# Rotary tables interleaved with two mixers, router logits moved into the layer norm, and smaller retention buffers

## The reference

```python
u = h @ ev_w_in[j]                       # layer 0: xa, ya | q, k, v, g
out_a = rg_lru_mixer(xa, ya, ...)        # conv, gates, scan over positions, gelu branch
out_b = retention_mixer(q, k, v, g, positions, gn_w)
...
def retention_mixer(q, k, v, g, positions, gn_w):
    q = rotary(q, positions); k = rotary(k, positions) * (RET_DIM ** -0.5)   # cos, sin of positions * inv_freq
    ...                                  # per head: chunk scores with decay, state recurrence over chunks
    o = head_group_norm(from_chunks(o_intra + o_inter), gn_w, RET_HEADS)
    return jax.nn.silu(g) * o
...
h = layer_norm(DEEPNORM_ALPHA * h + mix, ln_mix_g[i], ln_mix_b[i])
def hierarchical_moe(x, ...):
    group_logits = t @ w_group + b_group             # 4 columns
    expert_logits = einsum('td,gde->tge', t, w_router) + b_router    # 16 columns
    ...                                  # gate: one group, two of its four experts, softmax
```

## Time and profile before

| | us |
|---|---|
| median of six runs | 4342.27 (4284.7 to 4551.81) |
| the profiled execution | 4286.33 |
| its span on the slowest core (core 3) | 4284.8 |
| spans of the eight cores | 4266.7 to 4284.8 |
| load of x, layer 0 | 0 to 38 |
| rotary tables | 38 to 86 |
| loads, layer 0's mixers | 86 to 704 |
| reload of x, output projection and layer norm | 704 to 925 |
| router | 925 to 1024 |
| experts of layer 0 | 1024 to 1716 |
| router of layer 1 | 3228 to 3328 |

### The profile page before, as it was taken

How to read it: one execution, slowest core, us unless ns; L and a number is a source line. 1 busy time by engine, 2 the same in 40 slices (tenths; PEclk the granted TensorE clock), 3 DMA queues, 4 the chain that set the end, 5 groups by cost and what they waited for, 6 DMA issues and landing times.

```text
span 4284.8 us, 40588 instructions; the slowest of 8 cores (4266.7 to 4284.8 us)
## 1 busy us (share of the span) xinstructions
PE 2712.2 (63%) x12672; PEld 1312.2 (31%) x12672; DVE 1790.9 (42%) x2953; ACT 1173.3 (27%) x1880; POOL 1046.5 (24%) x857
## 2 busy tenths in 40 slices
PE   2544434619999999356534335555535999999646
PEld 1221222206444444122311112222215444444213
DVE  4233333322555555254432423333141455555344
ACT  1243332221111111342313125555230111111233
POOL 0323431131223232220123321111031223232130
PEclk6766766857999999678655556666765999999868
DMA  4010113020323231212000011001402122323201
GB/s 105 7 15 5 15 10 89 10 31 1 45 30 45 30 45 16 44 40 61 6 0 5 0 11 10 1 10 10 98 0 31 22 39 34 41 32 44 45 1 79
DMA packets 167293, 124.61 MB, mean 29 GB/s; under 512 B 62224, under 2 KB 143888, under 8 KB 166960
## 3 DMA queue, kind: packets, MB, share of 16 engines
q0 software_dynamic: 134352, 73.69, 13.6%
q1 hardware_dynamic: 32736, 48.33, 3.7%
HBM read 178.90 MB, written 16.78 MB: 46 GB/s over the span
## 4 chain that ended last, share of the span: by engine, by line
PE 54%; DVE 13%; DMA 9%; ACT 9%; POOL 8%; issue 7%; DVEq 0%; ACTq 0%; POOLq 0%; SPq 0%
PE psb L250 52%; POOL lnt L274 4%; DVE lnt L274 2%; ACT L270 2%; PE psb L254 2%; DMA ptok<-p 1%; DVE ssd_tmp L299 1%; DMA w_out<-od_w_out 1%; DMA xtok<-x 1%; POOL CdT L274 1%; DVE hg_kvall L299 1%; DMA wr_102<-moe_w_router 1%; DMA wr_255<-moe_w_router 1%; POOL MIX L274 1%; DMA wv<-ev_w_in 1%
## 5 line engine op out<-in xcount | busy, mean ns | idle before, releaser
L274 DVE TENSOR_TENSOR R<-R,psb 128x512 f32<-128x512 f32 x1088 | 664.5, 678 | 117.6 <-PE psb L250 117.6
L274 POOL TENSOR_TENSOR hm<-tm,gB 128x512 bf16<-128x512 f32 x256 | 325.5, 1271 | 1164.9 <-DVE tm L274 1164.9
L250 PE MATMUL psb<-HB,w1e 128*128 128x512 bf16 x2048 | 488.0, 381 | 0.0
L250 PE MATMUL psb<-HB,w3e 128*128 128x512 bf16 x2048 | 483.8, 379 | 0.0
L250 PE MATMUL psb<-hm,w2e 128*128 128x512 bf16 x2048 | 462.6, 379 | 0.0
L250 PEld LDWEIGHTS psb<-HB,w3e 128*128 128x128 bf16 x2048 | 200.4, 98 | 242.0 <-issue 0.7
L250 PEld LDWEIGHTS psb<-hm,w2e 128*128 128x128 bf16 x2048 | 200.4, 98 | 241.6
L250 PEld LDWEIGHTS psb<-HB,w1e 128*128 128x128 bf16 x2048 | 190.4, 98 | 242.9 <-issue 32.8
L274 POOL TENSOR_TENSOR lnt<-lnt,nmr 128x512 f32<-128x512 f32 x128 | 161.4, 1261 | 393.2 <-DVE lnt L274 393.2
L270 ACT ACTIVATE gB<-psb 128x512 f32<-128x512 f32 x128 | 76.4, 597 | 613.6 <-PE psb L250 613.6
L270 ACT ACT_TABLE_LOAD x136 | 174.5, 1283 | 179.5 <-PE psb L250 88.2
(11 more groups left out here) (381 smaller groups left out, 4172.7 us busy)
## 6 DMA issues: line engine op xcount, KB each, us to landing
xtok<-x SPq DMA_DIRECT2D x32, 512.0 KB, 5.5
w1e<-moe_w POOLq DMA_DIRECT2D x32, 512.0 KB, 6.1
w3e<-moe_w POOLq DMA_DIRECT2D x32, 512.0 KB, 8.8
w2e<-moe_w POOLq DMA_DIRECT2D x32, 512.0 KB, 11.2
r_spill<-R SPq DMA_DIRECT2D x4, 2048.0 KB, 7.3
R<-r_spill SPq DMA_DIRECT2D x4, 2048.0 KB, 34.8
out<-otok SPq DMA_DIRECT2D x16, 512.0 KB, 2.7
ptok<-p SPq DMA_DIRECT2D x32, 128.0 KB, 2.2
```

The costliest lines, as they stand in the source:

```text
L250: return self.op("pe", lambda e: e.matmul(out.ap, lhsT=lhsT.ap, rhs=rhs.ap, start=start, stop=stop), reads=[lhsT, rhs], writes=[out])
L274: return self.op(eng, lambda e: e.tensor_tensor(out=out.ap, in0=in0.ap, in1=in1.ap, op=op), reads=[in0, in1], writes=[out])
```

## The change

The rotary tables become a generator, `rotary_gen`, in four quarters of 512 tokens with 9 steps each, without a phase. `mixer_ret_gen` starts with it, so its 36 steps take turns with the first 36 steps of the LRU, and retention's own loads and heads come after them. To make room, `xb16`, `o_t` and `t3` become single tiles, and `sg` (2048 columns) goes: the g projection and its Silu move from the q and k loop into `_ret_gn`, one token tile at a time. The router's loads move ahead of `outproj_ln` (`router_setup`), and its matmuls into that pipeline, tile j-2 behind `ln_apply` of tile j-2 (`router_logits`); `moe_route` begins with the gate.

```diff
+def rotary_gen(self):
+    k = self.k
+    HS = SEQ // 4
+    self.cosT = k.sb([128, SEQ], F32, 4, "cosT")
+    self.sinT = k.sb([128, SEQ], F32, 4, "sinT")
...
+    for half in range(4):
+        hs = slice(half * HS, (half + 1) * HS)
+        k.dma("sp", posi.h[:], self.d["pos"][:, hs].partition_broadcast(128), writes=[posi.v()])
+        k.copy(ang.v(), posi.v())
+        k.ts(ang.v(), ang.v(), self.pcol("inv_freq"), ALU.mult)
+        yield
+        for shift, dst_t in ((math.pi / 2.0, self.cosT), (0.0, self.sinT)):
...
+            k.act(dst, dst, AF.Sin)
+            if dst_t is self.sinT:
+                k.ts(dst, dst, self.pcol("sin_sign"), ALU.mult)
+            yield
...
 def mixer_ret_gen(self):
...
+    yield from self.rotary_gen()
...
-    xb16 = [k.sb([128, 512], BF16, 1, "xb16") for _ in range(2)]
+    xb16 = [k.sb([128, 512], BF16, 1, "xb16")] * 2
...
-    sg = k.sb([128, SEQ], BF16, 4, "sg")
-    o_ts = [k.sb([128, 512], F32, 1, "o_t") for _ in range(2)]
+    sg = (k.sb([128, 512], BF16, 1, "sgj"), wg)
+    o_ts = [k.sb([128, 512], F32, 1, "o_t")] * 2
...
-            ps = self.proj(wg, 0, j)
-            k.act(sl(sg, j), ps.v(), AF.Silu)
...
     k.tt(c.v(), c.v(), b.v(), ALU.mult, eng="pool")
-    k.stt(self.MIXv(4 + hd, j), c.v(), self.pcol("ret_gnw", hd), sg.v(sg.h[:, j * 512:(j + 1) * 512], j), ALU.mult, ALU.mult)
+    sgj, wg = sg
+    ps = self.proj(wg, 0, j)
+    k.act(sgj.v(), ps.v(), AF.Silu)
+    k.stt(self.MIXv(4 + hd, j), c.v(), self.pcol("ret_gnw", hd), sgj.v(), ALU.mult, ALU.mult)
...
             self.ln_apply(j - 2, g, b, ga, ba, tmp)
+            self.router_logits(j - 2)
...
+def router_logits(self, j):
+    k = self.k
+    wr, bias, L = self.router_st
+    for tt in range(4 * j, 4 * j + 4):
         ps = k.ps()
         for kc in range(8):
             k.mm(ps.v(ps.h[:, 0:20]), self.R.v(self.R.h[:, kc, tt * 128:(tt + 1) * 128], self.rs(kc, tt // 4)),
                  wr.v(wr.h[:, kc, :]), start=(kc == 0), stop=(kc == 7))
-        k.stt(L.v(L.h[:, tt, :]), ps.v(ps.h[:, 0:20]), 1.0 / ALPHA, bias.v(), ALU.mult, ALU.add)
+        k.stt(L.v(L.h[:, tt, :], j), ps.v(ps.h[:, 0:20]), 1.0 / ALPHA, bias.v(), ALU.mult, ALU.add)
...
             self.reload_R()
+        self.router_setup(i)
         with k.phase():
             self.outproj_ln(i)
...
     if i % 2 == 0:
-        self.rotary_tables()
         run_interleaved([self.mixer_ret_gen(), self.mixer_lru_gen()])
```

More of the change, by code:

```diff
@@ L665, in rotary_tables @@
 def rotary_tables(self):
+    for _ in self.rotary_gen():
+        pass
+@_prog_method
+def rotary_gen(self):
     k = self.k
[L667 to L700, removed]
@@ new lines, in rotary_gen @@
+    HS = SEQ // 4
+    self.cosT = k.sb([128, SEQ], F32, 4, "cosT")
+    self.sinT = k.sb([128, SEQ], F32, 4, "sinT")
+    posi = k.sb([128, HS], I32, 1, "posi")
+    ang = k.sb([128, HS], F32, 1, "ang")
+    a2 = k.sb([128, HS], F32, 1, "a2")
+    kf = k.sb([128, HS], F32, 1, "kf")
+    for half in range(4):
[5 more added lines that the diff above has]
+        for shift, dst_t in ((math.pi / 2.0, self.cosT), (0.0, self.sinT)):
+            dst = dst_t.v(dst_t.h[:, hs], half)
+            if shift != 0.0:
+                k.ts(a2.v(), ang.v(), shift, ALU.add)
+                src = a2
+            else:
+                src = ang
+            k.ts(kf.v(), src.v(), 1.0 / TWO_PI, ALU.mult)
+            k.copy(posi.v(), kf.v())
+            k.copy(kf.v(), posi.v())
+            yield
+            k.stt(dst, kf.v(), -CW1, src.v(), ALU.mult, ALU.add)
+            k.stt(dst, kf.v(), -CW2, dst, ALU.mult, ALU.add)
+            yield
+            k.ts(kf.v(), dst, math.pi, ALU.is_gt, -TWO_PI, ALU.mult)
+            k.tt(dst, dst, kf.v(), ALU.add)
+            k.ts(kf.v(), dst, -math.pi, ALU.is_lt, TWO_PI, ALU.mult)
+            k.tt(dst, dst, kf.v(), ALU.add)
+            yield
+            k.ts(dst, dst, PI_SAFE, ALU.min, -PI_SAFE, ALU.max)
+            k.act(dst, dst, AF.Sin)
+            if dst_t is self.sinT:
+                k.ts(dst, dst, self.pcol("sin_sign"), ALU.mult)
+            yield
@@ L739, in mixer_ret_gen @@
     t2 = [k.sb([128, 512], F32, 1, "t2") for _ in range(2)]
-    t3 = [k.sb([128, 512], F32, 1, "t3") for _ in range(2)]
+    t3 = [k.sb([128, 512], F32, 1, "t3")] * 2
     scm4 = [k.sb([128, 4, 128], BF16, 1, "scm4") for _ in range(2)]
@@ L770, in mixer_ret_gen @@
         for j in range(NT):
-            cs = self.cosT.v(self.cosT.h[:, j * 512:(j + 1) * 512])
-            sn = self.sinT.v(self.sinT.h[:, j * 512:(j + 1) * 512])
+            cs = self.cosT.v(self.cosT.h[:, j * 512:(j + 1) * 512], j)
+            sn = self.sinT.v(self.sinT.h[:, j * 512:(j + 1) * 512], j)
             for (w0, dst) in ((wq, qr), (wk, kr)):
@@ L949, in moe_route, with router_setup @@
 @_prog_method
-def moe_route(self, i, gT):
+def router_setup(self, i):
     k = self.k
@@ L959, in moe_route @@
     k.dma("sp", bias.h[:], dd["moe_bias"][i:i + 1, :].partition_broadcast(128), writes=[bias.v()])
-    L = k.sb([128, NTT, 20], F32, 1, "L")
-    for tt in range(NTT):
+    L = k.sb([128, NTT, 20], F32, NT, "L")
+    self.router_st = (wr, bias, L)
+@_prog_method
+def router_logits(self, j):
+    k = self.k
+    wr, bias, L = self.router_st
+    for tt in range(4 * j, 4 * j + 4):
         ps = k.ps()
@@ L965, in moe_route @@
                  wr.v(wr.h[:, kc, :]), start=(kc == 0), stop=(kc == 7))
-        k.stt(L.v(L.h[:, tt, :]), ps.v(ps.h[:, 0:20]), 1.0 / ALPHA, bias.v(), ALU.mult, ALU.add)
+        k.stt(L.v(L.h[:, tt, :], j), ps.v(ps.h[:, 0:20]), 1.0 / ALPHA, bias.v(), ALU.mult, ALU.add)
+@_prog_method
+def moe_route(self, i, gT):
+    k = self.k
+    dd = self.d
+    wr, bias, L = self.router_st
     N = NTT
```

## The result

The changed kernel took 0.9907 of the time of the kernel before, 95% interval 0.9876 to 0.9938; its profiled execution took 4248.59 us beside 4286.33, where 4253 was predicted. Some executions of either kernel ran with one die at a lower granted clock; every ratio in this document leaves those out.

A forecast was written before the change was run, and what follows sets the result against it. Bound by stretches where engines wait for each other (rotary tables, router-weight load), not the matmul-filled MoE. From 4286.3 us: mixers +7, router -42 over two layers, w_out +2, giving 4253; range 4215 to 4292.

The forecast's parts named there:

- The start: First LRU projection at 84.7 us, 54.3 earlier, its small loads waiting only for two DVE passes and the memset.
- The price of the turns: LRU blocks beside retention: 67.5 us plus 0.65 per us of retention work; blocks 2 and 3 take 108.5 and 112.4.
- the fit of 0.65: Cost of one us of retention work beside an LRU block, fitted within 3 us to the earlier kernel's four blocks.
- the slower rival: Rival 5: turns in LRU blocks 2 and 3 hide nothing, +46 us, total 4299 us; chance 0.11.
- The tail: Retention alone for 68 steps instead of 29, 262 us; mixers end at 712 instead of 704.6, +7.
- Net +4 per head: Moving Silu into the group norm: 9.8 us more there, 6 less in the q and k loop, per head.
- 9.8 per head: Group norm longer by three logarithm table loads of 1.28 us and four Silu waits of 1.5 us.
- -6: Us saved per head when the g projection leaves the q and k loop.
- Rival 4: A table load holds ACT twice as long in the group-norm chain: 31 us, total 4284 us; chance 0.04.
- The router: Weights' load leaves the path, logits stay exposed in the layer norms; MoE starts 21 us earlier per layer.
- Not -86: Per layer, the 86 us of routing are not all saved, since MoE waits for expert weights and selb: only -21.
- w_out: Router weight transfers beside w_out's load cost 2 us in layer 0 (bounds 0 and 4), 0 in layer 1.

The follow-up runs named there:

- the version with the tables ahead: The changed kernel with the tables' 36 steps first and no barrier, then retention and LRU in turns: ratio 0.988, profiled 4249.0 us.
- the Silu run: The kernel before with only each head's gate projection and Silu moved into the group norm: ratio 0.9982 (0.9965 to 0.9999), profiled 4281.98 us.
- the second expert's run: The changed kernel with the second expert's weights loaded behind the route: ratio 0.9861, profiled 4225.17 us.
- the logits' run: The changed kernel with each tile's logits multiplied one tile of w_out later: ratio 0.9731, profiled 4174.34 us.
- the router alone: The kernel before with only the router's part of the change: ratio 0.9915 (0.9895 to 0.9934), profiled 4246.36 us.
- the tables ahead, with the loads' memset ahead of them: The changed kernel with the LRU's parameters and first loads issued first, then all tables without a barrier, then turns: ratio 0.979, profiled 4210.58 us.

## Why the prediction was right

**The start.** 84.7 predicted, 86.50 measured: the tables' DVE work did not hold the LRU's loads. That this hangs on the memset being early in DVE's order was one clause of the prediction; the version with the tables ahead shows it to be the condition.

**The price of the turns** came out in the sum and not block by block. Blocks 0 and 1, all but without ret: 148.0 for 144 (86.50 to 234.50). Block 2 took 125.2 for 108.5, block 3 from 359.71 to 461.0, where the LRU's last product ends, 101.3 for 112.4. So the fit of 0.65 was 0.92 in one block ((125.2 - 67.5) / 63) and 0.49 in the next ((101.3 - 67.5) / 69), 0.69 over both. The slope of 0.9 from which the slower rival decides was reached in block 2 alone. Block 2 takes 123.8 to 125.2 on all eight cores, so that this is no accident of one of them; what lies behind the spread was not tested.

**The tail.** 262 predicted, 249.6 measured (461.0 to 710.55). Most of the 12.4 is the rest of head 1: 49.0 us for 58, to 510.01, where the next head's wq is issued. The prediction let ret stand at the transposes of k; at 461.0 its recurrence had already run since 458.5. Two heads, counted from wq to wq and to the end (510.01, 609.60, 710.55), took 99.6 and 101.0 for 102.3. In them a size was off, "Net +4 per head". From its first v matmul the lone head takes 88.9 (621.64 to 710.55) for 88.3 before, +0.6; its weights landed 2.0 later behind wq's issue (12.0 for 10.0), and no run ties that to the Silu. The group norm, from its first o_t copy to the end, takes 41.9 for 36.3, 5.6 more and not "9.8 per head": the logarithm's load is paid in full in three tiles, but the Silu outlasts POOL's multiplication by 0.5 us a tile (2.01 for 1.51), where the prediction took 1.5, its price at half clock. What stands ahead of the group norm gives back 5.0 for "-6" (first v matmul to the first o_t 47.05 us, before 52.06). Beside the LRU the move is even a gain, as the Silu run shows, which the prediction did not have. Errors of +1.8, +4.0, +5.6 and -12.4 make the 710.55 for 712: the mixers' +5.9 for +7 owes something to luck.

**The table load.** It stays at 1283 ns over 59 loads, and the next pass starts 1.29 us and 1.30 us after the load's start (583.98 to 585.27, 586.73 to 588.03). **The Trainium skill** (ScalarE: Activation LUTs, What ACT_TABLE_LOAD costs) gives about 2.66 us with a drain. No drain is to be seen here. Rival 4 falls with the Silu run, whose interval ends below 1.

**The router.** Layer norms later by 20.3, 31 and 42 predicted; the first two came 19.0 and 29.6 later (874.87 and 916.99, less the 5.5 us by which w_out starts later, against 850.37 and 881.84 in the earlier trace rows). The MoE starts 22.9 and 23.2 us earlier for 21. That the load of the experts is what is left behind the last logits is shown by the second expert's run (-9.4 and -8.7), and that the logits are bare by the logits' run (-40.4 and -43.1; three tiles' logits are 32.5 of that, and the rest was not traced further). "Not -86" was right; where the rest went is these two.

**w_out** was to start 2 us later in layer 0; from the mixers' end it is 52.3, before 52.7: nothing. In layer 1 it started later by 4 in this pair of traces, but its load takes 44.8 with the router alone and 45.2 before, and 41.7 to 53.0 in the others: not the router's loads.

## What to carry to other kernels

An overlap that is only turns of two generators is spent by whoever stands in them: putting a third thing in front of one of them moves idle time, it doesn't remove it; here the tables ahead, with the loads' memset ahead of them, ended the mixers 43 to 46 us earlier than the interleaved ones (medians of eight cores, two runs) and took some 40 off the time. When a phase is fused into another to hide a load, look for what was hidden under the phase itself (here the experts' load) and for the order in which the fused matmuls meet the engine that feeds them. One tile of distance between producer and consumer was worth more than the fusing.

## What was unexpected in the hardware

The granted clock while the router's matmuls fill PE, in the changed kernel (columns as in the stretches above):

```profile
851.00:867.00 16.00, 15.87 (x67) 6.93 (x67) 5.02 (x9) 0.00 (x0) 0.00 (x0) 0.89 0.00 0
...
897.00:907.00 10.00, 10.00 (x49) 10.00 (x49) 0.53 (x3) 3.62 (x7) 0.98 (x2) 0.50 0.00 0
```

In 897 to 907 PE is busy throughout with fp32 matmuls of 128x20 and stays at 0.50, the level of 1.2 GHz; in the bf16 projection (851 to 867) the mean is 0.89. But the same fp32 matmuls do run at the upper level, 2.4 GHz, where they stand directly behind bf16 matmuls. With the logits late, tile 1's follow the statistics:

```profile
894.00:897.00 3.00, 3.00 (x29) 2.99 (x27) 1.02 (x2) 1.35 (x2) 0.00 (x0) 1.00 0.00 0
...
900.00:903.40 3.40, 3.40 (x17) 3.34 (x16) 1.77 (x4) 1.09 (x2) 1.27 (x1) 0.50 0.00 0
```

They start at 1.00, with 29 rows in 3.00 us, and are at 0.50, with 17 in 3.40, some 6 us later, though PE was busy with them all the while. Whether the type or the 20 columns brought it down no run here tells.

The same two halves of w_out landed in 41.7 us (logits late, 23.28 and 18.38) to 53.0 us (tables ahead, 27.48 and 25.50) in layer 1 of the slowest core: a spread of 11 us in the profiles that no edit explains; the second run of the same tables-ahead kernel took 43.4 (24.38 and 19.03).
